# Second attention, banded half: turns three iterations behind the scores, four probability rows, the sink as a column, output tiles begun between the last value steps

## The chip, the cores and the metric

The program runs on one core of one Trainium2 chip. The metric is the device time of one execution in microseconds. A core has five engines with a queue each, which the text calls by their short names: PE (TensorE, matrix products and transposes; PEld is its loading of weights), DVE (VectorE), ACT (ScalarE), POOL (GpSimd) and SP (SyncE, here only DMA). Each engine works through its own instructions in order; engines wait for one another by semaphores.

## The reference

The computation is a transformer of two blocks on 512 tokens of width 1024, float32. What matters here is one mixer of the second block. It has a global and a windowed attention, eight heads of 64 each, with two key and value heads; the windowed one has a learned sink per head:

```python
def windowed_gqa_sink(q, k, v, sink):      # per block of 128 queries, against the block before, its own, and the one after
    s = jnp.einsum('bnqkgd,bnskd->bnkgqs', qb, k_slab) * scale
    s = jnp.where(valid, s, NEG_INF)       # |qpos - kpos| <= 128, inside the sequence
    m = jnp.maximum(jnp.max(s, axis=-1), sk)
    p = jnp.exp(s - m[..., None])
    denom = jnp.sum(p, axis=-1) + jnp.exp(sk - m)
    p = p / denom[..., None]
    return jnp.einsum('bnkgqs,bnskd->bnqkgd', p, v_slab)

def even_mixer(...):
    ...
    return jnp.concatenate([oa, ob], axis=-1) @ w_out      # oa: global heads, ob: windowed heads
```

Ahead of it and after it stand feed-forward layers (width 2816), and the rest of the model, which the change doesn't touch.

## The kernel before

**Layout.** Activations lie with features on the 128 partitions and the 512 tokens along the row. Each matrix product is done in three passes (hi x hi, hi x lo, lo x hi; `PASSES`) of operands split in two parts: ACT copies a result out of PSUM as the hi part, DVE subtracts it from the result for the lo part. POOL does the same for weights: `split` (line 302) waits for a raw group of 128 x 1024 weights from DMA and for PE to be done with the group two before (`SPLIT` = 2 buffers), then runs L309 (one column, a spacer), L310 (hi) and L313 (lo). `group` (line 393) multiplies one such group, 24 matmuls on line 403.

**The second attention** (segment "even2_out") is one software pipeline of 32 iterations w and some more to drain. w = 0 to 15 is the global half, w = 16 to 31 the banded half (g = w // 16). In each, i = (w % 16) // 4 is a pair of heads ("two sides", one on each half of the partitions) and j = w % 4 a block of 128 queries. A banded w looks at two key chunks of 128 (j = 0, 3) or three (j = 1, 2); a global one at four. Four w make one head pair, called a head below.

For one w the work is: **scores** on PE (`scores_b`, L754) into two PSUM banks, `S_BANKS[w % 2]`; row maximum on DVE (global: L1668; banded: L1678 adds the window mask, writes the masked scores to a row pair of `tb` and takes the maximum, once per side, then L1682 makes the negated maximum of both sides and the sink); **exp** on ACT (L1194, with the row sum), and in the banded half the exp of the sink (L1200, two of 128x1); sum (banded, L1656) and **reciprocal** on DVE (L1658); scaling of both sides on POOL (L361); the **turn** on PE (`turn_b`, L768: transposes of each chunk into one of three PSUM banks `T_BANKS`); its hi part on ACT (L1183) and lo part on DVE (L1703), once per side. A **values step** (`values_b`, L786) is one side of one half head (two w): 12 matmuls in the global half, 9 in the banded. After four values steps a head is complete in PSUM bank 2; ACT copies it as `Y2` hi (L1173) and DVE makes its lo part (L1693), and the next head's first values step waits for that.

**The order** is written out by hand, one loop over w on each engine. In iteration w PE does scores w, turn w-2, and values step w-4. Scores wait for the exp of w-2. DVE does the reciprocal of w-1 first, then the maximum of w, then a completed head's lo part (w = 8, 12, 16, ...), then the two lo parts of w-2. ACT does a completed head's hi part, the hi parts of w-2, then the exp of w. POOL scales w; at w = 30 it first splits the weights of output tile 1. The masked scores of w go to the row pair `P_ROWS[w % 3]`, so DVE waits for the turn of w-3 before it writes them, and ACT before it writes the exp.

**After the loop** come eight output tiles: `group(m % 4, ...)` over all eight k-steps of `Y2`, and POOL splits tiles 2 to 7 in turn, each when the tile two before it is multiplied. `tail` on DVE and ACT adds each tile to x (L1525) and prepares the next layer. SP streams weights (L277) into four raw buffers, each reused when its split is done.

## Time and profile before

| | us |
| --- | --- |
| median of 3 runs | 2634.68 (2634.07 to 2640.07) |
| profiled execution, device time | 2636.19 |
| its span in the trace | 2634.4 |
| mean granted TensorE clock | 0.982 |
| PE / DVE / ACT / POOL busy | 2516.1 / 1116.1 / 623.3 / 1585.3 |

All times in the rows are microseconds from the start of the span, in one profiled execution. Busy time counts instructions at work on an engine; matmuls overlap one another by a fraction, so start-to-start distances are shorter than their durations. PEclk is the share of full speed (2.4 GHz) that was granted. "[x <-ENGINE line]" is idle time of the engine before the row, and what ended it.

### The profile page before, as it was taken

What the parts mean: (1) busy time and instruction counts of PE and PEld (TensorE: products, weight loads), DVE (VectorE), ACT (ScalarE), POOL (GpSimd) and SP (SyncE); (2) the same over time, 40 slices, a digit from 0 to 9 for tenths busy, and PEclk for the clock granted to TensorE, in tenths of its full rate; (3) what the DMA queues carried; (4) which work ended last, traced back from release to release, by engine and by line L of the source; (5) the groups of instructions that cost most, each with busy time, mean ns of one, the idle gap of its engine ahead of it and who ended that gap; (6) DMA issues with size and microseconds to landing.
All of it is one profiled execution on the core that took longest, in us unless ns stands there. A gap on an engine that the chain in (4) does not pass through costs nothing.

```text
span 2634.4 us, 32573 instructions
## 1 busy us (share of the span) xinstructions
PE 2516.1 (96%) x11718; PEld 2018.7 (77%) x11718; DVE 1116.1 (42%) x1491; ACT 623.3 (24%) x1196; POOL 1585.3 (60%) x1341
## 2 busy tenths in 40 slices
PE   7999788999999999988999999999998998999998
PEld 2777466888888886777888888888887787888886
DVE  4333765446333214576533323333213576533311
ACT  3221532112111102363211101111101565211100
POOL 1523145666666775434666677666675764666675
PEclk9999898999999999998999999999999999999999
DMA  6311542332323332101333333333332321333332
GB/s 230 137 35 56 176 152 79 97 96 96 96 96 96 99 108 73 60 1 39 102 98 98 97 104 103 97 96 96 103 103 81 97 74 41 95 97 100 97 104 80
DMA packets 68929, 249.07 MB, mean 95 GB/s; under 512 B 7536, under 2 KB 10096, under 8 KB 68208
## 3 DMA queue, kind: packets, MB, share of 16 engines
q1 hardware_dynamic: 63936, 232.81, 28.1%
q10 hardware_dynamic: 4912, 15.16, 1.6%
q8 instruction: 53, 0.87, 0.1%
q14 instruction: 28, 0.23, 0.0%
HBM read 245.85 MB, written 2.10 MB: 94 GB/s over the span
## 4 chain that ended last, share of the span: by engine, by line
PE 89%; DVE 5%; ACT 3%; issue 1%; POOL 1%; DMA 1%; SPq 0%; DVEq 0%; ACTq 0%; POOLq 0%
PE pb L403 70%; PE pb L891 3%; PE pb L834 2%; PE pb L637 1%; PE pb L577 1%; PE pb L786 1%; PE pb L877 1%; DVE tiny L1467 1%; PE pb L444 1%; PE pb L550 1%; PE pb L508 1%; PE pb L754 1%; ACT tb L1079 1%; PE pb L594 1%; PE pb L862 1%
## 5 line engine op out<-in xcount | busy, mean ns | idle before, releaser
L403 PE MATMUL pb<-ar,w_hi 128*128 128x512 f32 x5504 | 1708.1, 392 | 11.5 <-DVE ar L1342 4.3
L403 PEld LDWEIGHTS pb<-ar,w_hi 128*128 128x128 f32 x5504 | 1030.4, 188 | 243.1 <-issue 15.6
L403 PE MATMUL pb<-ar,w_lo 128*128 128x512 f32 x2752 | 1072.1, 390 | 0.0
L313 POOL TENSOR_TENSOR w_lo<-raw,w_hi 128x1024 fp32r<-128x1024 f32 x396 | 989.4, 2498 | 33.1
L403 PEld LDWEIGHTS pb<-ar,w_lo 128*128 128x128 f32 x2752 | 517.1, 188 | 108.8
L309 POOL TENSOR_TENSOR still<-still 128x1 f32<-128x1 f32 x396 | 79.4, 201 | 818.4 <-PE pb L403 607.0
L310 POOL TENSOR_SCALAR w_hi<-raw 128x1024 fp32r<-128x1024 f32 x396 | 420.7, 1062 | 0.0
L1604 DVE TENSOR_TENSOR tb<-pb,nb 128x512 f32<-128x512 f32 x88 | 60.9, 692 | 400.8 <-PE pb L403 400.8
L1525 DVE SCALAR_TENSOR_TENSOR x<-pb,x 128x512 f32<-128x512 f32 x48 | 36.5, 760 | 381.9 <-PE pb L403 381.9
L1610 DVE TENSOR_TENSOR ar<-tb,ar 128x512 f32 x88 | 154.8, 1759 | 92.4 <-ACT ar L1137 92.4
L1137 ACT ACTIVATE ar<-tb 128x512 f32 x88 | 55.7, 633 | 512.7 <-DVE tb L1607 512.7
L928 ACT ACTIVATE nb<-x 128x512 f32<-128x512 f32 x72 | 44.9, 625 | 381.2 <-DVE x L1525 375.6
L1135 ACT ACTIVATE tb<-tb 128x512 f32<-128x512 f32 x88 | 55.8, 634 | 248.3 <-DVE tb L1602 248.2
L1602 DVE TENSOR_TENSOR tb<-pb,nb 128x512 f32<-128x512 f32 x88 | 60.9, 692 | 91.1 <-PE pb L403 68.2
L1537 DVE SCALAR_TENSOR_TENSOR ar<-x,vec,ar 128x512 fp32r<-128x512 f32 x32 | 87.5, 2734 | 25.3 <-ACT ar L1098 25.3
L1607 DVE TENSOR_TENSOR tb<-tb 128x512 f32<-128x512 f32 x88 | 87.6, 995 | 11.5
L361 POOL TENSOR_SCALAR tb<-tb,tiny 128x512 f32<-128x512 f32 (+2 forms) x64 | 38.4, 613 | 79.8 <-DVE tiny L1658 79.8
L1300 DVE TENSOR_TENSOR nb<-nb 128x512 f32<-128x512 f32 (+1 forms) x70 | 72.4, 1034 | 21.0 <-ACT nb L928 19.6
L891 PE MATMUL pb<-ar,w_hi 128*128 128x512 f32 x256 | 80.8, 397 | 0.0
L1098 ACT ACTIVATE ar<-x,vec 128x512 fp32r<-128x512 f32 x32 | 23.2, 724 | 210.8 <-DVE x L1525 210.8
L340 POOL TENSOR_SCALAR tb<-tb,tiny 128x768 f32<-128x768 f32 x16 | 16.0, 1001 | 86.8 <-DVE tiny L1501 86.8
L786 PE MATMUL pb<-ar 128*128 128x256 f32 (+1 forms) x336 | 51.5, 307 | 13.1 <-DVE ar L1693 13.1
(203 smaller groups left out, 2282.2 us busy)
## 6 DMA issues: line engine op xcount, KB each, us to landing
raw<-wstream SPq DMA_DIRECT2D x444, 512.0 KB, 3.6
x<-xt ACTq DMA_DIRECT2D x2, 2048.0 KB, 9.6
tb<-dft ACTq DMA_DIRECT2D x1, 2048.0 KB, 10.9
out<-x ACTq DMA_DIRECT2D x8, 256.0 KB, 2.2
rt<-nbias ACTq DMA_DIRECT2D x4, 384.0 KB, 3.3
nb<-nbias ACTq DMA_DIRECT2D x4, 384.0 KB, 3.2
tb<-ctxt ACTq DMA_DIRECT2D x1, 1024.0 KB, 13.6
rt<-rope ACTq DMA_DIRECT2D x1, 1024.0 KB, 5.8
```

Source lines behind the costliest of these rows:

```text
L309: pool.tensor_tensor(still[:, 0:1], still[:, 1:2], still[:, 2:3], ALU.add)
L310: pool.tensor_scalar(w_hi[:, n % SPLIT, :], raw[:, j, :], 1.0, 1.0, ALU.mult, ALU.mult)\
L313: pool.tensor_tensor(w_lo[:, n % SPLIT, :], raw[:, j, :], w_hi[:, n % SPLIT, :].bitcast(F32), ALU.subtract).then_inc(s_split, 1)
L403: mm = pe.matmul(pb[:, bank, :], W[a][:, n % SPLIT, k * P:(k + 1) * P], rhs(b, k0 + k), start=(first and k == 0 and i == 0), stop=(last an ...
L786: mm = pe.matmul(pb[:, 2, q0 * P:q1 * P], E_VP[g][a][:, side, k, :], E_PT[side][b][:, k, q0 * P:q1 * P], start=(side == 0 and c == 0 and q ...
L891: mm = pe.matmul(pb[:, m % 2, :], W[a][:, m % SPLIT, k * P:(k + 1) * P], H[b][:, k, :], start=(k == 0 and i == 0), stop=(k == KT - 1 and i ...
L1300: dve.tensor_tensor(acc[:, 0:n], acc[:, 0:n], sq[k % 2][:, 0:n], ALU.add)\
L1537: dve.scalar_tensor_tensor(H[1][:, m, :], x[:, m, :], vcol(gain, i + m), H[0][:, m, :].bitcast(F32), ALU.mult, ALU.subtract)\
L1602: dve.tensor_tensor(tb[:, j, :], pb[:, 2 * j, :], rstd, ALU.mult).then_inc(s_ev, 1)
L1604: dve.tensor_tensor(tb[:, 4 + j, :], pb[:, 2 * j + 1, :], rstd, ALU.mult).then_inc(s_ev, 1)
L1607: dve.tensor_tensor(tb[:, 6 + j, :], tb[:, 2 + j, :], tb[:, 4 + j, :], ALU.mult)\
L1610: dve.tensor_tensor(tile(A_FFN[1], t * 2 + j), tb[:, 6 + j, :], tile(A_FFN[0], t * 2 + j).bitcast(F32), ALU.subtract)\
```

## The change

The diff covers the same segment only. On PE, DVE and ACT the turn of v stands in iteration v+2 for v < 14 and in v+3 from v = 14 on (`late`, `pair_late`); a values step s stands in s+4 or, from s = 14 on, s+5, and the first step of every head but the first one iteration later than that (`half_side`). The row pairs become four (`P_ROWS`), with the waits on the turn of w-3 becoming w-4. In the banded half the masked scores end at column `SINK` (384) of their row, and POOL writes the sink into column 384 two iterations ahead (`sinks`), so that L1194's exp covers it and its row sum contains it; the separate exps (L1200) and the addition (L1656) are gone. Banded scores wait for the maximum of w-2 and not its exp. On DVE the reciprocal of w-1 stands behind the maximum of w from w = 17 on. The split of tile 1's weights is done in two halves on POOL at w = 5 and w = 9 (`split_half`). Output tiles 0 and 1 are multiplied in pieces (`out_piece`): six of eight k-steps of tile 0 at w = 34, ahead of the last two values steps, then three of tile 1, the last two of tile 0, the last five of tile 1.

```diff
@@ -178,14 +178,25 @@
         T_BANKS = (3, 6, 7)
         C_BANKS = (4, 5)
         CT_BANKS = (2, 3, 6)
-        P_ROWS = ((5, 3), (0, 1), (2, 4))
+        P_ROWS = ((5, 3), (0, 1), (2, 4), (6, 7))
+        SINK = 3 * P
+
+        def late(v):
+            return 2 if v < 14 else 3
+
+        def pair_late(w):
+            return [v for v in (w - 3, w - 2) if 0 <= v < 32 and v + late(v) == w]
+
+        def half_side(w):
+            return [s for s in (w - 6, w - 5, w - 4)
+                    if 0 <= s < 32 and s + 2 + late(s) + (s > 0 and s % 4 == 0) == w]
         V_BANKS = (2, 7)
         PASSES = ((0, 0), (0, 1), (1, 0))
         W = (w_hi, w_lo)
...
@@ -314,6 +325,35 @@
                                    ALU.subtract).then_inc(s_split, 1)
             masks = rt[:, 0:3, :].rearrange("p a b -> p (a b)")
+
+            def split_half(g, n, half):
+
+                j, cols = n % RAW, slice(half * TOK, (half + 1) * TOK)
+                pool.wait_ge(s_raw[j], 16 * (g // RAW + 1))
+                pool.wait_ge(s_group, n - SPLIT + 1)
+                pool.tensor_tensor(still[:, 0:1], still[:, 1:2], still[:, 2:3], ALU.add)
+                ins = pool.tensor_scalar(w_hi[:, n % SPLIT, cols], raw[:, j, cols], 1.0, 1.0, ALU.mult, ALU.mult)
+                if half == 0:
+                    ins.then_inc(s_half, 1)
+                    pool.wait_ge(s_half, 1)
+                else:
+                    ins.then_inc(s_hi, 1)
+                    pool.wait_ge(s_hi, n + 1)
+                ins = pool.tensor_tensor(w_lo[:, n % SPLIT, cols], raw[:, j, cols], w_hi[:, n % SPLIT, cols].bitcast(F32),
+                                         ALU.subtract)
+                if half == 1:
+                    ins.then_inc(s_split, 1)
+
+            def sinks(w):
+
+                if w >= 16 + 4:
+                    pool.wait_ge(bt["e"], 2 * (w - 4) + 2)
+                else:
+                    pool.wait_ge(bt["t"], 2 * (w - 4) + 2)
+                for side in range(2):
+                    h = 4 * side + (w % 16) // 4
+                    pool.tensor_tensor(tb[:, P_ROWS[w % 4][side], SINK:SINK + 1], vcol("sink", h), still[:, 1:2],
+                                       ALU.add).then_inc(bt["sink"], 1)
             def bias_mask(w):
@@ -352,12 +392,14 @@
                 if seg == "even2_out":
                     split(g0, n0)
                     for w in range(32):
-                        if w == 30:
-                            split(g0 + 1, n0 + 1)
+                        if w in (5, 9):
+                            split_half(g0 + 1, n0 + 1, (w - 5) // 4)
                         n = TOK if w < 16 else P * len(chunks_of(w % 4))
+                        if 14 <= w < 30:
+                            sinks(w + 2)
                         pool.wait_ge(bt["r"], w + 1)
                         for side in range(2):
-                            p = tb[:, P_ROWS[w % 3][side], 0:n]
+                            p = tb[:, P_ROWS[w % 4][side], (0 if w < 16 else SINK - n):(n if w < 16 else SINK)]
                             pool.tensor_scalar(p, p, tiny[:, 40 + 2 * (w % 4) + side:41 + 2 * (w % 4) + side], 1.0,
                                                ALU.mult, ALU.mult).then_inc(bt["p"], 1)
                     for i in range(2, groups):
@@ -745,8 +787,10 @@
             def scores_b(w):
                 g, i, j = pair_b(w)
-                if w >= 2:
+                if 2 <= w < 18:
                     pe.wait_ge(bt["e"], 2 * (w - 2) + 2)
+                elif w >= 18:
+                    pe.wait_ge(bt["mx"], w - 1)
                 lo, hi = (0, 4) if g == 0 else (chunks_of(j)[0], chunks_of(j)[-1] + 1)
                 for q, (a, b) in enumerate(PASSES):
                     for side in range(2):
@@ -764,9 +808,11 @@
                     pe.wait_ge(bt["p"], n + 1)
                     if n >= 3:
                         pe.wait_ge(bt["lo"], n - 2)
-                    for c in range(4 if g == 0 else len(chunks_of(j))):
+                    cs = 4 if g == 0 else len(chunks_of(j))
+                    off = 0 if g == 0 else SINK - cs * P
+                    for c in range(cs):
                         mm = pe.transpose(pb[:, T_BANKS[n % 3], c * P:(c + 1) * P],
-                                          tb[:, P_ROWS[w % 3][side], c * P:(c + 1) * P], ident)
+                                          tb[:, P_ROWS[w % 4][side], off + c * P:off + (c + 1) * P], ident)
                     mm.then_inc(bt["t"], 1)
@@ -792,7 +838,18 @@
             pe.wait_ge(s_ev, TILE0["even2"] + 10)
             pe.wait_ge(s_qlo, 17)
-            for w in range(32 + 4):
+            def out_piece(m, k0, k1):
+
+                arrived(SPL0["even2_out"] + m)
+                for k in range(k0, k1):
+                    pe.wait_ge(bt["ylo"], k + 1)
+                    for i, (a, b) in enumerate(PASSES):
+                        mm = pe.matmul(pb[:, m, :], W[a][:, (SPL0["even2_out"] + m) % SPLIT, k * P:(k + 1) * P],
+                                       Y2[b][:, k, :], start=(k == 0 and i == 0), stop=(k == KT - 1 and i == 2))
+                if k1 == KT:
+                    mm.then_inc(s_group, 1)
+
+            for w in range(32 + 5):
                 if w == 16:
                     pe.wait_ge(s_qlo, 22)
                 if w < 32:
@@ -805,17 +862,20 @@
                     turn_v(1)
                 if w == 3:
                     pe.wait_ge(s_vlo, 6)
-                if 2 <= w < 34:
-                    turn_b(w - 2)
-                if w >= 4:
-                    values_b((w - 4) // 2, w % 2)
-
-            for m in range(8):
+                for v in pair_late(w):
+                    turn_b(v)
+                for s in half_side(w):
+                    values_b(s // 2, s % 2)
+                if w == 34:
+                    pe.wait_ge(bt["mx"], 31)
+                    out_piece(0, 0, 6)
+
+            out_piece(1, 0, 3)
+            out_piece(0, 6, KT)
+            out_piece(1, 3, KT)
+            for m in range(2, 8):
                 bank_free(TILE0["even2_out"] + m)
-                if m == 2:
-                    pe.wait_ge(bt["ylo"], 8)
-                group(m % 4, SPL0["even2_out"] + m, lambda b, k: Y2[b][:, k, :],
-                      (lambda k: pe.wait_ge(bt["ylo"], k + 1)) if m == 0 else None)
+                group(m % 4, SPL0["even2_out"] + m, lambda b, k: Y2[b][:, k, :])
             ffn("ffn1")
             ffn("ffn2")
@@ -1166,13 +1226,13 @@
                                    pb[:, V_BANKS[i], :].rearrange("p (k c) -> p k c", k=4)[:, :, cols], ACT.Copy)\
                         .then_inc(s_vhi, 1)
-            for w in range(32 + 5):
-                if w >= 8 and w % 4 == 0:
-                    head = (w - 8) // 4
-                    act.wait_ge(bt["o"], 2 * head + 2)
-                    act.activation(Y2[0][:, head, :], pb[:, 2, :], ACT.Copy).then_inc(bt["yhi"], 1)
-                if 2 <= w < 34:
-                    v = w - 2
+            for w in range(32 + 6):
+                for s in half_side(w - 1):
+                    if s % 4 == 3:
+                        head = s // 4
+                        act.wait_ge(bt["o"], 2 * head + 2)
+                        act.activation(Y2[0][:, head, :], pb[:, 2, :], ACT.Copy).then_inc(bt["yhi"], 1)
+                for v in pair_late(w):
                     j = v % 4
                     c0, cs = (0, 4) if v < 16 else (chunks_of(j)[0], len(chunks_of(j)))
                     if v % 2 == 0 and v >= 4:
@@ -1187,18 +1247,18 @@
                     g, j = w // 16, w % 4
                     n = TOK if g == 0 else P * len(chunks_of(j))
                     act.wait_ge(bt["mx"], w + 1)
-                    if w >= 3:
-                        act.wait_ge(bt["t"], 2 * (w - 3) + 2)
+                    if w == 3:
+                        act.wait_ge(s_vt, 2)
+                    if g == 1:
+                        act.wait_ge(bt["sink"], 2 * (w - 16) + 2)
+                    elif w >= 4:
+                        act.wait_ge(bt["t"], 2 * (w - 4) + 2)
                     for side in range(2):
-                        p, col = tb[:, P_ROWS[w % 3][side], 0:n], 2 * (w % 4) + side
+                        p, col = tb[:, P_ROWS[w % 4][side], (0 if g == 0 else SINK - n):(n if g == 0 else SINK + 1)], \
+                            2 * (w % 4) + side
                         act.activation(p, pb[:, S_BANKS[w % 2][side], 0:n] if g == 0 else p, ACT.Exp,
                                        bias=tiny[:, 8 + col:9 + col], accum_out=tiny[:, 16 + col:17 + col])\
                             .then_inc(bt["e"], 1)
-                    if g == 1:
-                        for side in range(2):
-                            h, col = 4 * side + (w % 16) // 4, 2 * (w % 4) + side
-                            act.activation(tiny[:, 24 + col:25 + col], tiny[:, 8 + col:9 + col], ACT.Exp,
-                                           bias=vcol("sink", h)).then_inc(bt["es"], 1)
                 if w in (0, 2):
                     v_hi(w // 2)
@@ -1649,16 +1709,10 @@
             def reciprocals(v):
                 c = 2 * (v % 4)
                 dve.wait_ge(bt["e"], 2 * v + 2)
-                total = tiny[:, 16 + c:18 + c]
-                if v >= 16:
-                    dve.wait_ge(bt["es"], 2 * (v - 16) + 2)
-                    b = 36 + 2 * (v % 2)
-                    link(dve.tensor_tensor(tiny[:, b:b + 2], total, tiny[:, 24 + c:26 + c], ALU.add))
-                    total = tiny[:, b:b + 2]
-                dve.reciprocal(tiny[:, 40 + c:42 + c], total).then_inc(bt["r"], 1)
-
-            for w in range(32 + 5):
-                if 1 <= w < 33 and w != 2:
+                dve.reciprocal(tiny[:, 40 + c:42 + c], tiny[:, 16 + c:18 + c]).then_inc(bt["r"], 1)
+
+            for w in range(32 + 6):
+                if 1 <= w < 17 and w != 2:
                     reciprocals(w - 1)
                 if w < 32:
                     g, i, j, c = w // 16, (w % 16) // 4, w % 4, 2 * (w % 4)
@@ -1672,28 +1726,30 @@
                         n, first = P * len(cs), (cs[0] - j + 1) * P
                         if w == 16:
                             dve.wait_ge(s_ld["wmask"], 16)
-                        dve.wait_ge(bt["t"], 2 * (w - 3) + 2)
+                        dve.wait_ge(bt["t"], 2 * (w - 4) + 2)
                         b = 32 + 2 * (w % 2)
                         for side in range(2):
-                            link(dve.tensor_tensor_reduce(tb[:, P_ROWS[w % 3][side], 0:n],
+                            link(dve.tensor_tensor_reduce(tb[:, P_ROWS[w % 4][side], SINK - n:SINK],
                                                           pb[:, S_BANKS[w % 2][side], 0:n], wm[:, first:first + n],
                                                           1.0, -3.0e38, ALU.add, ALU.max,
                                                           tiny[:, b + side:b + side + 1]))
                         dve.scalar_tensor_tensor(tiny[:, 8 + c:10 + c], tiny[:, b:b + 2], -1.0, minus_sink[:, :, i],
                                                  ALU.mult, ALU.min).then_inc(bt["mx"], 1)
+                if 17 <= w < 33:
+                    reciprocals(w - 1)
                 if w == 1:
                     v_lo(0)
                     reciprocals(1)
                     v_copy(1)
                 if w == 3:
                     v_lo(1)
-                if w >= 8 and w % 4 == 0:
-                    head = (w - 8) // 4
-                    dve.wait_ge(bt["yhi"], head + 1)
-                    dve.tensor_tensor(Y2[1][:, head, :], pb[:, 2, :], Y2[0][:, head, :].bitcast(F32),
-                                      ALU.subtract).then_inc(bt["ylo"], 1)
-                if 2 <= w < 34:
-                    v = w - 2
+                for s in half_side(w - 1):
+                    if s % 4 == 3:
+                        head = s // 4
+                        dve.wait_ge(bt["yhi"], head + 1)
+                        dve.tensor_tensor(Y2[1][:, head, :], pb[:, 2, :], Y2[0][:, head, :].bitcast(F32),
+                                          ALU.subtract).then_inc(bt["ylo"], 1)
+                for v in pair_late(w):
                     j = v % 4
                     c0, cs = (0, 4) if v < 16 else (chunks_of(j)[0], len(chunks_of(j)))
                     for side in range(2):
```

## Rows read from the trace of the kernel before

**Rows 1.** The page, parts 1 and 5: engines, and the costliest groups of instructions
```profile
PE 2516.1 (96%) x11718; PEld 2018.7 (77%) x11718; DVE 1116.1 (42%) x1491; ACT 623.3 (24%) x1196; POOL 1585.3 (60%) x1341
...
L361 POOL TENSOR_SCALAR tb<-tb,tiny 128x512 f32<-128x512 f32 (+2 forms) x64 | 38.4, 613 | 79.8 <-DVE tiny L1658 79.8
```

**Rows 2.** Table by stretch: length, busy us of each engine, PEclk, DMA share, GB/s
```profile
1151.78:1169.82 18.04, 13.53 (x112) 11.47 (x111) 13.03 (x46) 12.81 (x41) 5.52 (x10) 0.99 0.00 1
1169.82:1185.52 15.70, 12.59 (x80) 10.84 (x81) 9.83 (x38) 9.69 (x34) 4.15 (x8) 0.79 0.00 1
1185.52:1200.24 14.72, 11.31 (x80) 9.54 (x81) 9.81 (x38) 9.70 (x34) 4.16 (x8) 0.88 0.00 1
1200.24:1216.44 16.20, 11.28 (x75) 9.28 (x75) 10.49 (x33) 8.75 (x31) 7.54 (x11) 0.82 0.12 34
1216.44:1222.97 6.53, 6.53 (x40) 6.53 (x41) 1.63 (x4) 0.77 (x2) 0.13 (x1) 0.68 0.00 0
```

**Rows 3.** Timeline of PE, banded half: start, us, line, tiles, shape, count
```profile
1190.48 0.79 PE L754 MATMUL pb<-ar 64*128 64x384 f32 x6
1191.21 0.66 PE L768 MATMUL pb<-mat,tb 128*128 128x128 f32 x4
1191.62 1.24 PE L786 MATMUL pb<-ar 128*128 128x256 f32 x9
1192.79 0.62 PE L754 MATMUL pb<-ar 64*128 64x256 f32 x6
1193.34 0.87 PE L768 MATMUL pb<-mat,tb 128*128 128x128 f32 x6
1193.97 1.25 PE L786 MATMUL pb<-ar 128*128 128x256 f32 x9
...
1200.24 2.15 PE L786 MATMUL pb<-ar 128*128 128x256 f32 x9 [2.62 <-DVE ar L1693]
```

**Rows 4.** Timeline of PE, values steps of global heads
```profile
1125.56 1.66 PE L786 MATMUL pb<-ar 128*128 128x256 f32 x12 [1.01 <-DVE ar L1693]
...
1154.85 1.66 PE L786 MATMUL pb<-ar 128*128 128x256 f32 x12 [1.43 <-DVE ar L1693]
1156.43 0.79 PE L754 MATMUL pb<-ar 64*128 64x384 f32 x6
1157.16 1.09 PE L768 MATMUL pb<-mat,tb 128*128 128x128 f32 x8
```

**Rows 5.** Chain that ended last, from 1178 us: start, us, what
```profile
1178.38 1.31 ACT tb L1194 x4
1179.69 0.38 ACT tiny L1200 x2
```

**Rows 6.** Groups by line and shape, DVE, 1155 to 1216 us
```profile
L1678 DVE CUSTOM_DVE_ANT_0 tb<-pb,nb 128x384 f32<-128x384 f32 x16 | 8.9, 558 | 7.5 <-PE pb L754 7.1
L1703 DVE TENSOR_TENSOR ar<-pb,ar 128x384 fp32r<-128x384 f32 x14 | 7.1, 546 | 0.0
L1678 DVE CUSTOM_DVE_ANT_0 tb<-pb,nb 128x256 f32<-128x256 f32 x14 | 6.0, 425 | 0.6 <-issue 0.3
L1703 DVE TENSOR_TENSOR ar<-pb,ar 128x256 fp32r<-128x256 f32 x14 | 5.2, 415 | 0.0
L1656 DVE TENSOR_TENSOR tiny<-tiny 128x2 f32<-128x2 f32 x16 | 4.1, 258 | 11.7 <-ACT tiny L1200 11.5
L1693 DVE TENSOR_TENSOR ar<-pb,ar 128x512 fp32r<-128x512 f32 x4 | 2.7, 685 | 0.1
```

**Rows 7.** Line L1682 alone: ns min/median/max
```profile
L1682 DVE SCALAR_TENSOR_TENSOR tiny<-tiny x16: 161/161/542, 1153.6 to 1213.2; 128x2 f32<-128x2 f32 x16
```

**Rows 8.** Timelines of DVE and POOL: splits of output weights
```profile
1210.40 1.73 DVE L1656 TENSOR_TENSOR tiny<-tiny 128x2 f32<-128x2 f32 x1 [1.15 <-ACT tiny L1200]
...
1228.82 0.19 POOL L309 TENSOR_TENSOR still<-still 128x1 f32<-128x1 f32 x1 [12.25 <-PE pb L403]
...
1234.26 0.19 POOL L309 TENSOR_TENSOR still<-still 128x1 f32<-128x1 f32 x1 [1.75 <-PE pb L403]
```

More of the change, by code:

```diff
@@ L187, in build @@
         s_raw = [sem(f"raw_loaded{i}") for i in range(RAW)]
-        s_hi = sem("w_hi_split")
+        s_hi, s_half = sem("w_hi_split"), sem("w_hi_half_split")
         s_still = sem("still_zero")
@@ L218, in build @@
                                             "oln", "ors", "y", "yhi", "ylo")}
-        bt = {n: sem("attn2_" + n) for n in ("s", "mx", "e", "es", "r", "p", "t", "hi", "lo", "o", "yhi", "ylo")}
+        bt = {n: sem("attn2_" + n) for n in ("s", "mx", "e", "sink", "r", "p", "t", "hi", "lo", "o", "yhi", "ylo")}
         ct = {n: sem("attn3_" + n) for n in ("s", "mx", "e", "p", "t", "hi", "lo", "o", "yhi", "ylo", "qk_hi", "bm", "r")}
```

## The prediction

> **What bounds the kernel now.** I read the page's busy times first: TensorE (PE) is busy in 96% of the span [rows 1], so a change elsewhere pays only where PE stands idle or runs at its lower clock. Then I read the stretches of the second attention in the table by stretch [rows 2]. The banded half begins when the scores of w = 16 start (1151.78 us) and ends when output tile 0 starts (1222.97 us): 71.2 us. In the first four of its five stretches PE was idle for 18.04 - 13.53 = 4.5, then 3.1, 3.4 and 4.9 us, 15.9 us in all, and the granted clock fell from 0.99 to 0.79, 0.88, 0.82 and, in the last stretch, 0.68.
>
> The PE timeline gives each step at full clock, from start to start [rows 3]: scores 0.73 us over three key chunks and 0.55 over two; a turn (both sides of one w) 0.63 over three and 0.41 over two; one values step 1.17 to 1.18. Global values take 1.58 (1154.85 to 1156.43), and a global turn 1.09 of work less 0.25 that such a group overlaps the next, 0.84 [rows 4]. After an idle time of 2.62 us the same nine value matmuls are busy for 2.15 us instead of 1.24 [rows 3], 1.73 times as long: in that stretch the clock is partly at its 1.2 GHz level, not at 2.4. After idle times of 1.01 and 1.43 us nothing slowed down [rows 4].
>
> Full-clock work of the 71.2 us is then: scores 8 x 0.73 + 8 x 0.55 = 10.2; turns 2 x 0.84 + 8 x 0.63 + 8 x 0.41 = 10.0; values 4 x 1.58 + 16 x 1.18 = 25.2; together **45.4 us**. The other 25.8 us are 15.9 idle and 9.9 of lower clock. That is the most that this half can give back.
>
> Why PE waits is read from the chain of waits [rows 5]: mask and maximum on DVE, exp on ACT (1.31), sink exp on ACT (0.38), sum and reciprocal on DVE, and only then the next mask. DVE works in order, and L1656, the first thing of its iteration, waited 11.5 us for ACT in this stretch [rows 6], so one w costs 3.0 to 3.7 us where PE's own work is about 2.35. A head's period in rows 2 is 14.7 to 16.2 us.
>
> **The change, part by part.** (a) *Order on DVE.* From w = 17 the reciprocal of w-1 stands behind the mask of w, so the loop mask, exp, reciprocal, mask is cut: mask w+1 runs while ACT does exp w. DVE then has per w: two masks, 2 x 0.60 us over three chunks or 2 x 0.47 over two (0.56 and 0.42 of work [rows 6], and 0.04 that I add for the link), L1682 and the reciprocal some 0.35 with their gaps (L1682 is 0.16 [rows 7]), two lo parts of 0.5 or 0.38 (0.55 and 0.42 of work, overlapping a little [rows 6]), some 0.07 of waits. Over the four w of a head: 4.3 + 1.4 + 3.5 + 0.3 = 9.5, plus 0.65 for the head's lo (L1693, 0.69 [rows 6]): **10.1 us of DVE** against 9.4 us of PE (2 x 0.73 + 2 x 0.55 + 2 x 0.63 + 2 x 0.41 + 4 x 1.18). DVE becomes the fuller engine, narrowly. ACT was busy 9.7 us in a head [rows 2]; without its sink exps (4 x 0.38 [rows 5]) 8.2. The column makes each exp one element longer, nothing to measure.
>
> (b) *Turn three iterations behind, four rows.* The turn of w-3 needs p of w-3, whose reciprocal was made an iteration earlier: POOL's 1.2 us (2 x 0.61 [rows 1]) lies under it. The fourth row pair lets mask w wait for turn w-4, already passed. Scores now wait for the maximum of w-2, not its exp: never late.
>
> (c) *First values of a head one iteration later.* Head copy and its lo no longer stand between two values steps; but from w = 21 on, lo of w-3 is queued on DVE behind mask w and the head's lo, and PE's second turn of the next iteration waits for it. I followed one head, with T the end of its last values step. PE: scores and turn to T+1.4, scores to 2.1, first side of the turn to 2.3. DVE: masks from 0.7 to 1.9, L1682 and reciprocal to 2.2, head lo to 2.9 (its ACT copy, begun at T, is done by then), first lo at 3.4, so PE goes on at T+3.6: idle 1.2 to 1.3. Two values steps to 6.1, then scores, turn, values, twice, with no wait over 0.1: next T at **10.6 us**. Before it was 15.7, 14.7 and 16.2 [rows 2].
>
> (d) *The start.* w = 16 has scores alone. Scores 17 wait for exp 15 (idle 0.2), values 12 and 13 for the head's lo (0.7), the second side of turn 16 for the lo of 15 behind the three-chunk mask of 18 (0.9). Values 16 start 17.7 us after scores 16 (18.0 before), but with scores of two more w and a turn behind them.
>
> (e) *The drain.* Three periods on, values 28 would start at 17.7 + 31.8 = 49.5. The last period has no scores or mask of w = 32 and 33 (0.5 off PE, 1.6 off the wait): 47.4. Four values steps follow, 4.7: **52.1 us**, of which 6.7 idle, against 71.2. Output piece 0 (18 matmuls of 5.44 / 24 = 0.227 us [rows 8], 4.1 us) is work moved forward; it stands where lo 30 and 31 are finished and hides the wait for them, and the first steps of piece 1 (2.0 us) hide the last head's copies on ACT and DVE (about 2 x 0.65 us). Cover gone, those 1.3 us would be paid.
>
> (f) *POOL.* The split of tile 1 leaves w = 30, where POOL's 3.7 us held back a scale and stretched L1656 on DVE to 1.73 us [rows 8]. Its halves (about 1.9 us each) at w = 5 and 9 go in front of a scale; POOL is idle 79.8 / 32 = 2.5 us before a pair of scales [rows 1], so I cost them at 0, at most 1. The sink columns are two POOL instructions per w, costed like L309 of the same shape at 0.2 us [rows 8]: with 4.2 us busy in a head before [rows 2] POOL has 5.8 of 10.6 us. ACT now waits for them. They stand behind the scale of w-3 in the queue; the loop exp, reciprocal, scale, sink, exp is 1.3 + 1.6 + 1.2 + 0.4 = 4.5 us for three iterations of 2.6 each, so it doesn't bind. L1656 disappears, L1682 remains open to a POOL instruction in progress (0.54 at worst beside 0.16 [rows 7]: bound 0.4 x 16 = 6 us, lowest 0; I take 0, since the scale starts just after L1682 and ends before the next).
>
> SBUF — State Buffer, "SBUF: two separate sides", in the Trainium skill says a DVE instruction with two SBUF inputs and a GpSimd one exclude each other for a whole instruction. By that rule the 1.73 us of L1656 is a wait for POOL's split, and the new sink columns can hold L1682 up too: it would take up to those 6 us from the sum, where my reading of the order takes none.
>
> (g) *Global half.* The two waits of 1.01 us for the head's lo ([rows 4] has the one at w = 8; that at w = 12 is like it) shrink to about 0.35: 1.3 us gained.
>
> (h) *Output tiles.* Tiles 0 and 1 now end 15 matmuls (3.4 us) apart. POOL can split tile 2 only when tile 0 is done; tiles were 1234.26 - 1228.82 = 5.44 us apart, of which POOL idled 1.75, so a split takes 3.7, and it began 0.4 us after tile 0's last matmul (1222.97 + 5.44 = 1228.41) [rows 8]. 0.4 + 3.7 + 0.1 - 3.4: PE waits **0.8 us**, where before it had 1.3 to spare. Loads on SP's queue for these groups are only released earlier.
>
> **Sum.** 71.2 - 52.1 = 19.1, plus 1.3, minus 0.8: 19.6 us. Against the profiled execution's 2636.2 us that is 2616.6; the median of the runs is 1.5 us lower, 2634.7, so **2615 us**. A measurement here can tell about 0.3%, 8 us, from no change.
>
> **Rivals.**
> *PE's clock dips all the same.* In rows 3 the slow stretch followed 2.62 us of idling, and 1.4 us did no harm [rows 4]; but the changed half has small waits together with weaker PE load. One dip costs 0.9 us on its first values step [rows 3] and about as much again on what follows, some 2.3 us a head (the present half lost 9.9 in four heads and the drain), and makes PE late so that DVE has a little less to be waited for: 3 or 4 dips leave a gain of 11 to 14, 2622 us. TensorE: Matmul & The Clock Gate, Part 4, in the Trainium skill says that transposes don't count as activity as matmuls do; the stretch of scores and turns at the head change would then weigh more, for this rival. No row here isolates it.
>
> *DVE sets a slower pace.* If each w costs DVE 0.3 us more than I added (a POOL instruction met at L1682, a late link), 16 x 0.3 = 5 us are lost: 2620 us. For it: L1682 has taken 0.54 us once beside 0.16 [rows 7]. Against: the new order puts it clear of POOL.
>
> *Hardly a wait left.* If the head's lo is ready earlier than I have it, up to 5 of the 6.7 idle us go: 2610 us.
>
> *Slower than before: the banded half at 1.2 GHz throughout.* If the small waits keep the clock at its lower level from w = 16 on, the 45.4 us of work take 1.73 times as long, 78.5 us, with the waits hidden beneath: 7.3 us over 71.2, less 0.5 of the rest, 2642 us. The sign turns once more than 19.6 / (0.73 x 45.4) = 59% of the work runs low. Against it: the global half, with a 1.01 us wait per head, was not slowed [rows 4], and even the present half with its 2.6 us idle times recovers within each head.
>
> *The change doesn't do what it says:* the loop of ACT and DVE comes back through a wait I judged idle (the sink column, the turn of w-4 in front of the mask); then periods stay near 14 us, 2631 us.
>
> **How the numbers follow.** My sum, give or take 3 us: 57%. Clock dips 15%, slower DVE pace 13%, hardly a wait 6%, loop still closed 5%, slower than before 4%. The range leaves out the last two and the outermost of the first rivals: 2609.5 to 2623.5. Faster by over 0.3% takes all but the last two: 0.91; within 0.05; slower 0.04.
>
> **What would show it.** Right: banded half near 52 us plus 4.1 of output piece; heads 10 to 11 us apart; DVE above 90% busy there; one PE wait of about 1.2 us per head ended by the lo line; PEclk near 1.0; no ACT-to-DVE wait at the reciprocal; a wait of 0.8 us for POOL before output tile 2. Wrong: PEclk under 0.9 there, periods of 12 us or more, PE waiting for POOL in turns, or ACT waiting for the sink column.

## The result, and the profile after

| | before | changed |
| --- | --- | --- |
| median, first comparison | 2635.4 us (4 runs) | 2613.6 us (4 runs, 2609.2 to 2617.9) |
| ratio, 95% interval | | 0.9915 (0.9901 to 0.9928) |
| the same two kernels again, another comparison | 2634.9 us (7 runs) | 2613.6 us (4 runs), 0.9917 (0.9901 to 0.9934) |
| span of the profiled execution | 2634.4 us | 2612.3 us |

The change takes 21 to 22 us away, 0.8%; both intervals lie clear below 1. The forecast was 2615, within 2609.5 to 2623.5.

The table by stretch of the changed kernel answers to [rows 2]. Columns are the stretch, its length, busy time of each engine, PEclk, DMA share and GB/s. The stretches are w = 4 to 15, w = 16 to the last values step, and from there to output tile 2.

```profile
1104.71:1146.83 42.12, 41.85 (x313) 34.55 (x313) 33.72 (x52) 31.52 (x79) 21.02 (x34) 0.97 0.05 14
1146.83:1201.51 54.68, 50.34 (x403) 43.52 (x403) 38.36 (x139) 35.83 (x107) 22.24 (x62) 1.00 0.00 1
1201.51:1209.15 7.64, 7.06 (x33) 5.53 (x32) 3.84 (x3) 1.84 (x3) 3.74 (x4) 1.00 0.01 2
```

The banded half, 71.2 us before, is 54.7 us, and 4.1 of these are output piece 0 (1195.33 to 1199.47 in the timeline). So 50.5 us are left for the same work. PE idles for 4.3 us where it idled for 15.9, and its granted clock is 1.00 where it was 0.79 to 0.88 in the heads.

One head of the changed kernel in the timeline of PE answers to [rows 3] (start, us, line, shape, count, idle time before it; L798 scores, L814 turn, L832 values):

```profile
1164.05 0.41 PE L814 MATMUL pb<-mat,tb 128*128 128x128 f32 x2 [0.81 <-DVE ar L1759]
1164.22 2.29 PE L832 MATMUL pb<-ar 128*128 128x256 f32 x18
1166.44 0.63 PE L798 MATMUL pb<-ar 64*128 64x256 f32 x6
...
1172.46 0.80 PE L798 MATMUL pb<-ar 64*128 64x384 f32 x6
1173.19 0.44 PE L814 MATMUL pb<-mat,tb 128*128 128x128 f32 x2
1174.43 0.41 PE L814 MATMUL pb<-mat,tb 128*128 128x128 f32 x2 [0.80 <-DVE ar L1759]
1174.59 2.29 PE L832 MATMUL pb<-ar 128*128 128x256 f32 x18
```

The first values step of a head starts at 1164.22, the next head's at 1174.59: 10.37 us. The one wait in between stands at the second side of the turn, and a lo part on DVE (L1759) ends it. Who waits for whom has changed too; of the waits from 1148 to 1206 us (engine and line, releaser, us in total, times, longest):

```profile
DVE tb L1732 <- PE pb L798: 6.4, 10, 1.5
ACT tb L1259 <- DVE tiny L1736: 3.9, 5, 1.2
PE pb L814 <- DVE ar L1759: 3.4, 4, 1.0
DVE tiny L1712 <- ACT tb L1259: 0.4, 1, 0.4
```

DVE waited 11.5 us for the sink exp ahead of the addition and the reciprocal [rows 6]; now it waits 0.4 us for the exp there. For PE's scores it waited 7.1 us in 4 waits and now waits 6.4 us in 10, so in most iterations PE's scores come last now. PE sets the pace again. Output tile 2 has the wait that the forecast gave it, in the timeline of all engines: POOL begins the split at 1205.32, PE starts on it at 1209.15:

```profile
1205.32 0.19 POOL L320 TENSOR_TENSOR still<-still 128x1 f32<-128x1 f32 x1 [14.00 <-PE pb L847]
...
1209.15 0.70 PE L445 MATMUL pb<-ar,w_hi 128*128 128x512 f32 x2 [0.58 <-POOL w_lo L324]
```

**Where the 22 us came from.** Starts in the PE timelines give: w = 4 to 16, 44.4 before, 42.1 after; scores 16 to tile 0 or to the last values step less piece 0, 71.2 and 50.5; output tiles 0 and 1, 11.0 (1222.97 to 1233.95) and 4.1 + 7.6 = 11.8. That is 2.3 + 20.7 - 0.8 = 22.2 us. The spans differ by 22.1 us too, but that agreement is chance: ahead of w = 4 the changed execution was 2.6 us shorter, and behind the start of output tile 2 it was 2.7 us longer (1403.2 against 1400.5 us). In the second profile of the changed kernel the same two parts were 1.2 us longer and 0.3 us shorter than before.

### The profile page after: what moved, and what is told of

Its sections match the earlier page's. It is cut to its first block, busy times and chain, and to the rows that moved or that the text cites. A ratio compares the mean times of both kernels' runs of the same rounds, so it can differ in the third digit from the quotient of the medians.

```text
span 2612.3 us, 32547 instructions
## 1 busy us (share of the span) xinstructions
PE 2511.1 (96%) x11718; PEld 2014.3 (77%) x11718; DVE 1112.6 (43%) x1475; ACT 617.7 (24%) x1164; POOL 1591.1 (61%) x1376
## 4 chain that ended last, share of the span: by engine, by line
PE 91%; DVE 5%; ACT 2%; issue 1%; POOL 1%; DMA 1%; SPq 0%; ACTq 0%; DVEq 0%; POOLq 0%
PE pb L445 71%; PE pb L951 3%; PE pb L894 2%; PE pb L679 1%; PE pb L832 1%; PE pb L619 1%; PE pb L937 1%; PE pb L486 1%; DVE tiny L1527 1%; PE pb L592 1%; PE pb L550 1%; PE pb L814 1%; DVE ar L1405 1%; PE pb L798 1%; PE pb L922 1%
## 5 line engine op out<-in xcount | busy, mean ns | idle before, releaser
L445 PE MATMUL pb<-ar,w_hi 128*128 128x512 f32 x5472 | 1699.0, 392 | 10.1 <-DVE ar L1402 5.0
L1667 DVE TENSOR_TENSOR tb<-tb 128x512 f32<-128x512 f32 x88 | 87.7, 996 | 11.5
L1360 DVE TENSOR_TENSOR nb<-nb 128x512 f32<-128x512 f32 (+1 forms) x70 | 72.4, 1035 | 21.1 <-ACT nb L988 19.6
## 6 DMA issues: line engine op xcount, KB each, us to landing
tb<-ctxt ACTq DMA_DIRECT2D x1, 1024.0 KB, 13.4
```

Source lines behind the costliest of these rows:

```text
L445: mm = pe.matmul(pb[:, bank, :], W[a][:, n % SPLIT, k * P:(k + 1) * P], rhs(b, k0 + k), start=(first and k == 0 and i == 0), stop=(last an ...
L1360: dve.tensor_tensor(acc[:, 0:n], acc[:, 0:n], sq[k % 2][:, 0:n], ALU.add)\
L1667: dve.tensor_tensor(tb[:, 6 + j, :], tb[:, 2 + j, :], tb[:, 4 + j, :], ALU.mult)\
```

## The experiments

Each kernel's three numbers come from its PE timeline: the **stretch** from scores 16 to output tile 2, which contains everything of the banded half and the two tiles; the **fill**, from scores 16 to the first values step of the first banded head; and the **heads**, the distances of those first steps. The changed kernel gave 62.32 us and 62.35 us in two profiled executions, while single executions of one kernel lie up to 10 us apart as wholes (2630.0 to 2640.0 us for the kernel before). Every other kernel has one profile. Where PE waits for about 2 us or more, in the kernel before and in d, g, i and j, its clock may fall or not (last section), so these stretches could come out 1 to 4 us different in another execution (my estimate, from the prices given there); differences of 1 us among the others stand on one profile against two. The medians are given as well.

| kernel | stretch | fill | heads | heads to tile 2 | median |
| --- | --- | --- | --- | --- | --- |
| before | 82.17 | 18.0 | 15.7, 14.7, 16.2 | 17.5 | 2635 |
| changed (z_after) | 62.35 | 17.4 | 10.4, 10.4, 8.2 | 16.0 | 2613.6 |
| reciprocal ahead again (a) | 63.44 | 17.7 | 10.7, 10.7, 8.4 | 16.0 | 2617.0 |
| sink exps again (b) | 63.29 | 17.8 | 10.6, 10.6, 8.4 | 16.0 | 2616.3 |
| both of these (i) | 74.93 | 20.2 | 13.2, 13.4, 12.1 | 16.0 | 2626.0 |
| turns two behind (c) | 62.69 | 15.8 | 10.5, 10.5, 9.9 | 16.0 | 2616.8 |
| no extra iteration (d) | 66.97 | 19.7 | 11.0, 11.0, 8.9 | 16.4 | 2620.0 |
| c and d together (n) | 65.12 | 16.0 | 11.2, 11.1, 10.5 | 16.4 | 2623.5 |
| before, reciprocal behind (g) | 68.87 | 16.3 | 11.5, 11.5, 12.4 | 17.1 | 2624.2 |
| changed, without the order on DVE, c and d (j) | 70.76 | 16.0 | 12.2, 13.1, 11.5 | 18.0 | 2624.9 |
| tiles 0 and 1 after the loop (e) | 61.57 | 17.4 | 10.4, 10.4, 8.2 | 15.2 | 2615.4 |
| split of tile 1 at w = 30 (f) | 63.14 | 17.4 | 10.4, 10.4, 9.0 | 16.0 | 2615.0 |
| e, scores ahead at heads (m) | 59.53 | 17.4 | 9.7, 9.7, 7.6 | 15.2 | 2612.2 |

Medians of b, d, e, f, j and n are of one run each.

### The changed kernel again

> The changed kernel once more, as the yardstick of this group. From the first scores of w = 16 to the end of the last values step, less output piece 0: 50.5 us in its first profile; heads 10.4 us apart; 2.3 us less than before between w = 4 and w = 16; output tile 2 waits 0.6 us for POOL. If part of the 22 us lay in places that the change does not touch (the first profile had 2 us less ahead of w = 2), this one shows less than 22 us.

2613.6 us, ratio 0.9917 (0.9901 to 0.9934), stretch and heads as in the first profile. From w = 4 to 16 it took 41.3 us, 3.1 less than before instead of 2.3. The difference lies in the first turn after a wait of 3.15 us at w = 3, which neither kernel avoids, and in the clock there.

### Reciprocal ahead of the mask again

```diff
-                if 1 <= w < 17 and w != 2:
+                if 1 <= w < 33 and w != 2:
                     reciprocals(w - 1)
...
-                if 17 <= w < 33:
-                    reciprocals(w - 1)
```

> The changed kernel with the reciprocal of w-1 ahead of the mask of w again. Theory 1 (the loop mask, exp, reciprocal, mask is what bound the half, and its cutting is the gain): the loop is back, less the sink's 0.38 + 0.19 us, 2.7 to 2.9 us per w; heads 11.5 to 12 us apart, the half 5 to 7 us longer, DVE waiting for ACT at the reciprocal. Theory 2 (shortening the loop by the sink's instructions was enough): heads within 0.3 us of 10.4. Theory 3 (the depth of three iterations was the gain): the same as theory 2.

Stretch 63.44 us: 1.1 us longer, not 5 to 7, heads 10.7. The waits show the loop is back, though barely binding (DVE's reciprocal for ACT's exp, ACT's exp for DVE's maximum, waited for by nearly every w):

```profile
ACT tb L1259 <- DVE tiny L1736: 8.5, 15, 1.2
DVE tiny L1712 <- ACT tb L1259: 6.4, 14, 0.7
```

My figure for the loop was wrong by the two-chunk iterations. A three-chunk w costs 1.20 for the masks, 0.2 for L1682, 1.31 for the exps, 0.17 for reciprocal and links, 2.88 us; a two-chunk w 2.40. A head is then 10.6 us, and 10.70 was measured; PE needs 10.4 anyway. Taken alone, this result speaks for theories 2 and 3. The next ones tell them apart.

### The kernel before, with the reciprocal behind the mask

```diff
-                if 1 <= w < 33 and w != 2:
+                if 1 <= w < 17 and w != 2:
                     reciprocals(w - 1)
...
+                if 17 <= w < 33:
+                    reciprocals(w - 1)
                 if w == 1:
                     v_lo(0)
```

> The kernel before with one change: the reciprocal of w-1 behind the mask of w in the banded half. Theory 1: the heads come from 14.7 to 12.5-13 us apart, 6 to 8 us gained over the half, and PE then waits for POOL's scale in the turns. Theory 2 (sink) and theory 3 (depth): under 2 us gained; it may even lose, since the scale starts later and turns are only two behind.

Moving this one call in the old kernel brings the stretch from 82.2 to 68.9 us, heads from 14.7 to 11.5: two thirds of the whole gain, with turns two behind, three row pairs and the sink's exps in place. That is 13.3 us, where I had expected 6 to 8 and heads of 12.5 to 13. Its median is 2624.2 us, ratio 0.9956 (0.9939 to 0.9973), 10.7 us less than before: by whole executions it is half of the 21.2 us, which include the global half. The idle times at heads shrink from 2.98 and 2.62 to 1.4 us, and after them the values step runs at full speed. The waits for POOL's scale that I had expected in the turns only draw out two turns of each head by 0.24 us (1.11 us instead of 0.87, 0.90 instead of 0.66). One long wait is left: behind POOL's split at w = 30 PE waits 2.62 us (2.49 in the kernel before), and after that it doesn't run at full speed (timeline of PE):

```profile
1181.45 1.23 PE L786 MATMUL pb<-ar 128*128 128x256 f32 x9 [1.37 <-DVE ar L1695]
...
1204.42 1.32 PE L768 MATMUL pb<-mat,tb 128*128 128x128 f32 x6 [2.62 <-POOL tb L361]
1205.39 2.16 PE L786 MATMUL pb<-ar 128*128 128x256 f32 x9
```

### Sink exps and addition back

```diff
-                        if 14 <= w < 30:
-                            sinks(w + 2)
...
+                    if g == 1:
+                        for side in range(2):
+                            h, col = 4 * side + (w % 16) // 4, 2 * (w % 4) + side
+                            act.activation(tiny[:, 24 + col:25 + col], tiny[:, 8 + col:9 + col], ACT.Exp,
+                                           bias=vcol("sink", h)).then_inc(bt["es"], 1)
...
+                total = tiny[:, 16 + c:18 + c]
+                if v >= 16:
+                    dve.wait_ge(bt["es"], 2 * (v - 16) + 2)
+                    b = 36 + 2 * (v % 2)
+                    link(dve.tensor_tensor(tiny[:, b:b + 2], total, tiny[:, 24 + c:26 + c], ALU.add))
+                    total = tiny[:, b:b + 2]
```

> The changed kernel with the sink's own exps on ACT and the addition on DVE back (and no sink column on POOL). Theory 1: with the loop cut these lie beside other work: 0.2 us more on DVE per w, heads 10.4 to 11 us apart, at most 3 us over the half. Theory 2 (the sink's instructions were the gain): heads 12.5 us or more.

63.29 us, 0.9 more than changed, heads 10.6, as theory 1 has it. The sink's work isn't the gain as long as the loop is cut elsewhere.

### Both cuts undone

The edit is that of a and b together.

> The changed kernel with both cuts of the loop undone: reciprocal ahead of the mask, and the sink's exps and addition back; depth of three, the head's extra iteration and four row pairs stay. Undone one at a time they cost 1.1 and 0.9 us from scores 16 to tile 2 (62.35 us). If the loop mask, exp, sink exp, addition, reciprocal is what binds (2 x 2.88 + 2 x 2.40 us for mask, exp and reciprocal of a head, plus 4 x 0.57 for the sink: 12.8 us), the heads are 12.8 us apart and the stretch is 70 to 73 us. If the gains simply add up, 64.4 us and heads 10.9 us apart.

74.93 us, heads 13.2 and 13.4. Undone singly the two cost 1.1 and 0.9 us, undone together 12.6. Ratio to before 0.9962 (0.9947 to 0.9976), so about three fifths of the gain have gone, though turns are three behind. The other 7.2 us (82.17 to 74.93) come with the cuts undone, from the parts that stay: depth, extra iteration, fourth row pair, scores that wait for the maximum, split and output pieces. No run here adds one of these alone to the kernel before. The chain of work that ended last shows the loop without any PE in it (start, us, what; L1728 masks, L1732 maximum, L1244 exp, L1250 sink exp, L1706 addition):

```profile
1182.30 0.56 DVE tb L1728
...
1182.90 0.56 DVE tb L1728
...
1183.51 0.17 DVE tiny L1732
...
1183.70 1.11 ACT tb L1244 x3
...
1185.10 0.29 ACT tiny L1250
...
1185.48 0.17 DVE tiny L1706
...
1185.80 0.42 DVE tb L1728
```

From mask to mask that is 3.50 us for a three-chunk w. The sum for a head was 12.8, and 13.2 and 13.4 were measured. In each of these heads L1732 took 0.37 us once instead of 0.17 (1173.51, 1186.73) and ended with a scale on POOL; that is 0.2 of the 0.4 to 0.6 us on top, and the rest I can't place. The stretch is 2 us above the range that I had given, mostly by the clock: behind the last of the three waits at heads it was granted at 0.63 from 1194.60 to 1206.88 us, and the last head took 12.1 us against 8.2. Of the 12.6 us, 2.8 are the fill, 5.8 the first two heads and 3.9 this one.

### Sink column alone

The changed kernel with `late` returning 2, the head's extra iteration out, and the edit of a. Four row pairs, scores that wait for the maximum, the split at w = 5 and 9 and the output pieces stay too.

> The changed kernel with the reciprocal ahead of the mask, turns two behind and no extra iteration at heads: of the changes to the banded order only the sink column is left. If either cut of the loop is enough: the loop is 10.6 us per head plus a wait at the head as in the kernel with the reciprocal alone (11.5 us apart, 1.4 us idle): 11.5 to 12.5 us, stretch 68 to 71 us. If the order on DVE matters by itself: heads 13.5 us or more, 75 us.

70.76 us, heads 12.2, 13.1 and 11.5: either cut is enough to come most of the way, this kernel 11.4 us of 19.8 and the order on DVE 13.3. The 11.4 can't all be put down to the sink column, since w = 30 has no split ahead of it here. The head of 13.1 us shows what the clock adds (timeline of PE): after 1.99 us of idling, the second values step takes 2.16 us.

```profile
1180.41 1.23 PE L832 MATMUL pb<-ar 128*128 128x256 f32 x9 [1.99 <-DVE ar L1748]
...
...
1183.21 2.16 PE L832 MATMUL pb<-ar 128*128 128x256 f32 x9
```

### Turns two behind

```diff
         def late(v):
-            return 2 if v < 14 else 3
+            return 2
```

> The changed kernel with turns two iterations behind in the banded half too; row pairs, sink column and the order on DVE as changed. Theory 1: the reciprocal now comes after the mask, so the scale of w-2 ends about when PE reaches its turn: 0.3 to 0.6 us of waiting for POOL per w, heads 11.5 to 12.5 us. Theory 3: the depth is most of the gain, heads 13.5 us or more. Theory 2: heads near 10.4 us.

62.69 us: 0.3 more than changed, where I had expected 0.3 to 0.6 per w. PE does wait for POOL at the head's turn, as its timeline shows, but little:

```profile
1186.79 0.98 PE L814 MATMUL pb<-mat,tb 128*128 128x128 f32 x4 [0.35 <-POOL tb L403]
```

The heads cost 1.9 us more together (30.9 against 29.0), and the fill 1.5 less, since at w = 16 PE no longer has scores alone. So the third iteration of depth pays for itself and no more.

### No extra iteration ahead of a head's values

```diff
-                    if 0 <= s < 32 and s + 2 + late(s) + (s > 0 and s % 4 == 0) == w]
+                    if 0 <= s < 32 and s + 2 + late(s) == w]
```

> The changed kernel without the extra iteration ahead of a head's first values step. The global half gets its two waits for the head's lo back, 0.9 us each more than the changed kernel; in the banded half PE waits 1.5 to 1.8 us at the values step where it now waits 0.8 at the turn: heads 11 us apart, 3.5 to 5 us in all. Rival: in the banded half the two waits are the same one (DVE's queue), and only the 1.8 us of the global half come back.

4.6 us more in the stretch, heads 11.0, and 43.2 us instead of 41.3 from w = 4 to 16: 6.5 us by the trace, more than I had given it. Half of it is the fill, where the clock enters once more. The only work between scores 16 and values 12 is gone:

```profile
1148.22 0.62 PE L798 MATMUL pb<-ar 64*128 64x256 f32 x6
1151.30 2.90 PE L832 MATMUL pb<-ar 128*128 128x256 f32 x12 [2.46 <-DVE ar L1750]
```

Twelve value matmuls that take 1.66 us took 2.90.

### Both

The edits of c and d together.

> The changed kernel with turns two behind and without the extra iteration at heads; sink column and order on DVE stay. Undone alone, the depth cost 0.3 us and the extra iteration 4.6 (of 62.35). If the head's lo is what PE waits for and depth gives nothing: 67 us, heads 11.0 us apart. If depth and extra iteration stand in for each other: 69 us or more, heads 11.5 us.

65.12 us, less than with the extra iteration out alone (66.97): three behind without the extra iteration is worse than neither, by the fill (19.7 against 16.0). Neither of my two numbers was right.

### Output tiles 0 and 1 after the loop

```diff
-                if w == 34:
-                    pe.wait_ge(bt["mx"], 31)
-                    out_piece(0, 0, 6)
...
-            out_piece(1, 0, 3)
-            out_piece(0, 6, KT)
-            out_piece(1, 3, KT)
+            out_piece(0, 0, KT)
+            out_piece(1, 0, KT)
```

> The changed kernel with output tiles 0 and 1 whole, after the loop. My reading of its trace: the pieces fill no wait, since lo 31 is ready before values step 30 would start, and the first six steps of tile 0 (4.1 us) cover the last head's copies; and tile 2 has 5.4 us instead of 3.4 for its split. So 0.6 to 0.9 us less than the changed kernel from scores 16 to tile 2. The reason given in my prediction (the piece hides waits for lo 30 and 31, and the last copies) would cost 0.7 to 2 us.

61.57 us, 0.8 less than the changed kernel. The last values steps and the tiles run without a gap:

```profile
1195.73 4.38 PE L832 MATMUL pb<-ar 128*128 128x256 f32 x36
1199.95 0.67 PE L847 MATMUL pb<-ar,w_hi 128*128 128x512 f32 x2
```

These 36 matmuls are the four last values steps, 28 to 31. Nothing waited between them, so the piece put there hid nothing, and it cost the wait of tile 2.

### Split of tile 1 at w = 30

```diff
-                        if w in (5, 9):
-                            split_half(g0 + 1, n0 + 1, (w - 5) // 4)
+                        if w == 30:
+                            split(g0 + 1, n0 + 1)
```

> The changed kernel with the split of tile 1's weights in one piece at w = 30 on POOL. If POOL's 3.7 us is on the path: the scale of 30 comes 2 to 3.5 us late, PE waits that long at the turn of 30, and DVE may be held at L1736 while POOL is in the split. If three iterations of depth cover it: under 1 us.

0.8 us more in the stretch, all in the last head (9.0 against 8.2): PE waits for the scale of w = 30, but for 0.9 us and not 2 to 3.5, as I had it for the case that three iterations of depth cover it; it then waits less for the lo part.

```profile
1195.06 1.46 PE L814 MATMUL pb<-mat,tb 128*128 128x128 f32 x8 [0.89 <-POOL tb L403]
1196.93 0.41 PE L814 MATMUL pb<-mat,tb 128*128 128x128 f32 x2 [0.42 <-DVE ar L1759]
```

### Scores ahead at heads, on top of e

```diff
-                if w < 32:
+                if w < 32 and w not in (23, 27, 31):
                     scores_b(w)
...
                 for v in pair_late(w):
-                    turn_b(v)
+                    turn_b(v, (lambda: scores_b(w + 1)) if w in (22, 26, 30) else None)
```

`turn_b` calls this between its two sides.

> The changed kernel with tiles 0 and 1 whole after the loop, as in the run before (0.8 us less than the changed kernel), and the scores of w = 23, 27 and 31 put between the two sides of the turn ahead of them, where PE waits 0.8 us at each head. They fill 0.55 to 0.7 us of that wait: heads 9.8 us apart, 1.7 us less; stretch from scores 16 to tile 2 about 59.8 us against 62.35. If the lo parts on DVE move back by as much (DVE serves mask 23 earlier, ahead of nothing), the same; if a bank or the mask of 21 is late, the scores wait there and nothing is gained.

The heads are 9.7 us apart, the stretch 59.53 us, 2.0 less than e's and 2.8 less than the changed kernel's, and the wait at the head is 0.25 us:

```profile
1174.33 0.62 PE L798 MATMUL pb<-ar 64*128 64x256 f32 x6
1175.20 0.41 PE L816 MATMUL pb<-mat,tb 128*128 128x128 f32 x2 [0.25 <-DVE ar L1757]
```

Its median is 2612.2 us, 0.9910 of before (0.9890 to 0.9930). That it beats the changed kernel is shown in the stretch of its one trace alone; whole executions can't tell 2.8 us apart.

## Why the prediction was right, point by point

**The sum.** Forecast 19.6 us: 19.1 in the banded half, 1.3 in the global half, 0.8 lost at tile 2. The trace has 20.7, 2.3 and 0.8, together 22.2. The signs of the terms were right; the banded half was forecast 1.6 us too low and the global half 1.0.

**What bound the kernel** (the loop mask, exp, sink exp, addition, reciprocal): shown by g and i, and borne out by j. The order on DVE alone takes 13.3 of 19.8 us, j with the sink column 11.4, and undoing both cuts gives 12.6 back. What I hadn't said is that the two cuts replace each other: what runs a and b undo can't be summed, and undoing one is no measure of its worth.

**The clock.** Of the 25.8 us that the half could give back, I had put 9.9 down to the lower clock, and let them go with the long waits. That holds: PEclk is 1.00 in the changed half in both of its profiles, and of the 20.7 us gained 11.6 are idle time and 9.0 busy time, the lower clock's. An idle time of 1.44 us or less that stood alone slowed nothing in this attention in any kernel here. The rival of recurring dips doesn't occur, and neither does the half at 1.2 GHz.

**(a) DVE the fuller engine** was wrong. The term that failed first is "L1682 and the reciprocal some 0.35": they start 0.08 us apart and the lo part 0.07 to 0.08 after that (1162.62, 1162.70, 1162.77 in DVE's timeline of the changed kernel). DVE was busy for 8.6 us of a 10.4 us head, where I had 10.1, and for 38.4 of the 54.7 us of the half, 70%, where I had over 90%; in the half it waited 6.4 us for scores. The rival of a slower DVE went the other way.

**(c) The wait at a head** was the right wait at the right place, with 0.8 us instead of 1.2 to 1.3, for the same reason: DVE reaches the lo part earlier. A head came out at 10.37, not 10.6. PE was idle for 4.3 us in the half instead of 6.7 and busy for 0.8 us more than my 45.4, which makes the 1.6 us above the forecast.

**(b) Depth** earned nothing by itself (c: 0.3 us). I had charged POOL's scale as covered by it, rightly, but at depth two it is nearly covered as well.

**(d) The start** came out at 17.4 us, forecast 17.7. PE waited 0.55 us for the head's lo, 0.33 at the turn of 16, for POOL's scale and not for a lo part, and 0.81 at the turn of 19, for a lo part.

**(e) The drain** had its reason wrong. The piece of tile 0 hides no wait; e is 0.8 us faster without it. The wait for lo 30 stands ahead of values 28, before the piece, and stays (0.96 us).

**(f) POOL's halves** at w = 5 and 9 cost nothing visible: w = 5 to 8 are 3.34 us apart as before. Moving the split away from w = 30 is worth 0.8 us in the changed kernel, through the scale of w = 30. With turns two behind it may be worth more: in g, where the split stays, the last head is 12.4 us against 8.2. No run moved it alone. The sink columns are waited for by nobody. L1736, which replaces L1682, took 0.55 us once, at w = 16, and 0.16 otherwise, so the bound of 6 us that I took at nothing cost 0.4.

**(g)** was too small. The two waits of the global half cost 1.25 us each in spacing (4.59 against 3.34) and became 0.35 each: 1.8 us. I had taken the idle time of 1.01 for the price. The rest of the 2.3 is the clock after the wait at w = 3, which comes out differently from one execution to the next.

**(h)** was right: 0.8 forecast; e, which has no such wait, is 0.8 us shorter, and PE's idle time before tile 2 is 0.58 us.

## What to carry to other kernels

Look for the loop that an in-order queue closes between iterations: here a 0.17 us reciprocal stood ahead of the next mask, and moving it one place was worth 13 us of 82. When two edits cut the same loop, test them singly and together, since each alone looks worthless on top of the other. Work put into a gap has to be checked against the trace for the gap being there; of the two fillers tried here, the output piece filled none and the early scores filled 0.55 us per head.

## What the runs showed of the hardware

Whether an idle time of TensorE lowers its clock isn't settled by its length alone. In the second attention none of 1.44 us or less did that stood alone, but waits of 0.28, 0.58 and 1.34 us within 3.3 us did, in j's drain (PEclk 0.67 from 1205.03 to 1210.18); 1.99 us did once and once not (the second one of j, whose stretch has PEclk 1.00); in i, 2.27 us slowed the values behind it (18 matmuls in 3.14 us), 2.17 us, one head later, did not (2.30 us), and 2.27 us, another head later, slowed them more (4.08 us), each behind the same scores, turn, scores and half a turn:

```profile
1168.17 0.41 PE L801 MATMUL pb<-mat,tb 128*128 128x128 f32 x2 [2.27 <-DVE ar L1753]
1168.33 3.14 PE L819 MATMUL pb<-ar 128*128 128x256 f32 x18
...
1181.38 0.41 PE L801 MATMUL pb<-mat,tb 128*128 128x128 f32 x2 [2.17 <-DVE ar L1753]
1181.55 2.30 PE L819 MATMUL pb<-ar 128*128 128x256 f32 x18
...
1194.91 4.08 PE L819 MATMUL pb<-ar 128*128 128x256 f32 x18
```

So the price of a wait of 2 to 2.5 us is its length, or its length and another 1.2 us (d, twelve value matmuls) to 3.9 us (i, the last head).

The execution alone can decide. The third attention, which the change doesn't touch, has waits of 1.13 to 1.15 and 1.37 to 1.38 us that end 2.8 us apart, in all 14 profiles here. In nine of them the values step behind the second wait ran slow, in five it didn't, the kernel before among these. The changed kernel is on both sides, with its first profile (granted clock 0.50 from 2169.93 to 2175.93 us) and its second (1.00 from 2174.09 to 2180):

```profile
2169.93 2.15 PE L937 MATMUL pb<-ar 128*128 128x256 f32 x9 [1.37 <-DVE ar L1793]
...
2174.09 1.24 PE L937 MATMUL pb<-ar 128*128 128x256 f32 x9 [1.37 <-DVE ar L1793]
```

The page TensorE: Matmul & The Clock Gate, Part 4, in the Trainium skill says that transposes don't count as activity as matmuls do; the changed kernel has 2.7 us of scores and turns alone and a wait of 0.8 us at each head and was granted 1.00 throughout the banded half, so that rule made no difference here.

A small DVE instruction can last until a POOL instruction in progress ends. In the profile before, L1682 (128x2) took 0.16 us eleven times and 0.36 to 0.54 us five times, and each of the five ended 0.01 us after a scale of POOL. L1656's 1.73 us [rows 8] ended at 1212.13, with POOL's split:

```profile
1209.76 2.36 POOL L313 TENSOR_TENSOR w_lo<-raw,w_hi 128x1024 fp32r<-128x1024 f32 x1
```

So that 1.73 us was a wait for POOL in the middle of the loop. The masks (L1678), which read PSUM, kept their 0.42 us beside a scale (1212.76).
